# Weight splits a step later on DVE, earlier output half-steps, and hi-first products behind norms, in a fused attention and MoE kernel

## The chip, the cores and the metric

The kernel runs on one core of a Trainium2 chip. The metric is the device time of one execution in microseconds. TensorE (PE) does the matrix products, VectorE (DVE), ScalarE (ACT) and GpSimd (POOL) the rest, and SyncE (SP) issues most of the transfers.

## The reference

All in float32, for 256 tokens of width 1024. It is two blocks in a row.

The first has two layers, each attention and then a gated feed-forward net:

```
layer 0: fox attention, 8 heads (log-sigmoid forget sums added to the scores)
         dsa attention, 8 heads over a latent of 128, top 64 keys picked by an index score
layer 1: moba attention, 16 heads (one block of 256 keys, so plain causal attention here)
each:    x = x + mixed @ w_out;  x = x + (silu(conv3(g)) * u) @ w_down,  g, u = split(rmsnorm(x) @ w_up)
```

The second block is one layer:

```
c_q, c_kv, k_r, x_m, z, i, f = split(rmsnorm(x) @ w_in)
mla attention, 8 heads, from c_q and c_kv
mlstm, 4 heads: xc = silu(conv4(x_m)), q and k from xc, v from x_m, gates i and f
ml = (norm(hm) * g + skip * xc) * silu(z)
x = x + concat(mla, ml) @ w_o
x = x + MoE(rmsnorm(x)), 32 experts, top 2
x = x + (p @ w_ple) * sigmoid(rmsnorm(x) @ w_gate);  return rmsnorm(x)
```

## The kernel before

Five instruction streams are written out by hand, one per engine: `tensor` (PE), `scalar` (ACT), `vector` (DVE), `gpsimd` (POOL) and `sync` (SP). They meet through semaphores only, so the order within each stream is the order of the work. Tokens lie in two tiles of 128 (t = 0, 1); the width of 1024 is eight slices k of 128.

**Products in split precision.** SP brings each weight chunk (up to 1 MB) into a ring of slots. ACT rounds it to `wh` (`split_hi`, line 1249), DVE makes the rest `wl = w - wh` (`split_lo`, line 1757), each into one of three buffers. The other operand is split too: hh and hl of a norm, mh (`mix_hi`, ACT) and ml (`mix_lo`, DVE) of the heads' outputs. PE (line 525) adds three products: high by high, high by low, low by high. A ring slot is free when both splits have read it. `ahead()` is the generator by which ACT and DVE split some chunks ahead of PE.

**A norm.** `add_x` on DVE adds the output projection's banks to x. `norm_T` on PE transposes x (line 529) into four banks of PSUM, two slices k and two tiles t in each, and a bank is announced when it is full. ACT makes hh from it, DVE hl (line 1767). The norms are an0, fn0 (layer 0 and its net), an1, fn1, nm2 (block 2) and np2 (the final gate). `tok_steps` and `gemm_fm` are the products behind a norm; chunk c holds slices k = 2c and 2c+1.

**Head loops.** `for i in range(21)` in layers 0 and 1, `range(15)` in block 2. At step i PE does the scores of head i, a half chunk of the next projection (`next(proj)`), the transposes of head i−2's probabilities (`probs_T`), perhaps another half chunk, and head i−3's value product. `head_at` leaves steps 8 and 9 without a head. DVE does the maxima of step i (lines 1771 and 1762), ACT the exponentials (`probs`, line 1246) and copies of transposed probabilities (`evac_P`). In layers 0 and 1 the first eight heads' outputs are normalised (`finish`), transposed (`mixT`), split, and multiplied by the first half of the output weights in half steps (`out_steps`), while the second eight heads run. Layer 0 also has rotary work on POOL (line 2549) between `even_evac(4)` on ACT and the transposes `dqT` on PE. Block 2's loop mixes mla and mlstm heads; DVE's `ml_1` and `ml_2` are the parts of the latter, and `z_steps` places the half chunks of the z projection. Ahead of it come the products pj and xm, convolution taps on DVE (line 1767, form sA<-sA,cv), copies and Silu.

Banks of PSUM are given out by `claim` and by `take` in a `rotation`; a claim waits until the former content is drained.

## Time and profile before

| what | value |
|---|---|
| median of 3 runs | 1125.15 us (1123.03 to 1128.29) |
| the profiled execution, its time | 1126.01 us |
| its span in the trace | 1124.2 us |
| PE busy | 1056.7 us (94%) |
| DVE busy | 619.9 us (55%) |
| ACT busy | 522.5 us (46%) |
| POOL busy | 89.5 us (8%) |
| mean granted clock of PE | 0.965 |

Times in the trace are microseconds from the start of the span. Stages lie about so: layer 0 to 164, its net to 356, layer 1 to 491, the second net to 683, block 2's attention to 816, router and experts from there to 1090, then the final gate. A span of 40 slices gives PE a busy share of 0.9 or more in most of them; the low ones lie at the start, in the head loops and in block 2.

### The profile page before, as it was taken

To read this page: it belongs to the slowest core of one execution; us is meant where nothing else is said; L and a number is where in the kernel's file an instruction comes from. 1 tells how busy PE (TensorE), PEld (TensorE's weight loads), DVE (VectorE), ACT (ScalarE), POOL (GpSimd) and SP (SyncE) were. 2 spreads that over 40 slices of the span, in tenths; PEclk is the share of its full clock that TensorE was granted. 3 is DMA by queue.
4 is the path that set the end of the run, shared out by engine and by line. 5 is a ranking of instruction groups with operands and counts; after the bars stand their busy time and mean duration, and the time that the engine had idled before them with its cause. 6 is when DMAs were issued, how large, how long until landed. Compare 5 with 4: busy or idle time off the path is not lost.

```text
span 1124.2 us, 15541 instructions
## 1 busy us (share of the span) xinstructions
PE 1056.7 (94%) x6143; PEld 828.0 (74%) x6143; DVE 619.9 (55%) x1167; ACT 522.5 (46%) x901; POOL 89.5 (8%) x104
## 2 busy tenths in 40 slices
PE   6998899999999999999999998888989999999987
PEld 5776679999987877789999887678764544555445
DVE  4667356888845555567888647545672121221146
ACT  5654446555535454455555435655352222222155
POOL 0100000212100311001212101100000000000000
PEclk9998699999999999999999999989889999999989
DMA  8733044465565533246565564105628999999930
GB/s 285 272 113 113 1 142 156 155 200 173 190 199 172 187 118 108 76 133 192 164 192 183 191 186 136 76 13 182 229 107 323 409 409 408 409 409 408 406 129 38
DMA packets 112672, 224.63 MB, mean 200 GB/s; under 512 B 10559, under 2 KB 65234, under 8 KB 112594
## 3 DMA queue, kind: packets, MB, share of 16 engines
q1 hardware_dynamic: 112434, 223.04, 56.3%
q8 instruction: 51, 0.84, 0.3%
q10 hardware_dynamic: 160, 0.53, 0.1%
q14 instruction: 27, 0.22, 0.1%
HBM read 222.50 MB, written 1.05 MB: 199 GB/s over the span
## 4 chain that ended last, share of the span: by engine, by line
PE 81%; DVE 9%; ACT 4%; issue 2%; DMA 2%; SPq 1%; POOL 0%; DVEq 0%; ACTq 0%; POOLq 0%
PE ps L525 76%; PE ps L529 4%; DVE wl L1757 2%; ACT wh L1249 1%; DMA ring<-in_w_uv_dram 1%; DVE smb L1771 1%; DVE x L1757 1%; ACT pb L1246 1%; SPq L2627 1%; DMA ring<-in_w_in_even_dram 1%; DVE sA L1767 1%; DVE xs L1757 0%; DVE hl L1767 0%; SPq L2624 0%; ACT L1246 0%
## 5 line engine op out<-in xcount | busy, mean ns | idle before, releaser
L1757 DVE TENSOR_TENSOR wl<-ring,wh 128x1024 fp32r<-128x1024 f32 (+3 forms) x212 | 278.5, 1323 | 183.2 <-ACT wh L1249 182.5
L1249 ACT ACTIVATE wh<-ring 128x1024 fp32r<-128x1024 f32 (+3 forms) x212 | 222.7, 1053 | 155.5 <-PE ps L525 152.5
L525 PE MATMUL ps<-hh,wh 128*128 128x256 f32 x768 | 220.2, 287 | 3.7 <-DVE big L1762 2.3
L525 PE MATMUL ps<-hh,wl 128*128 128x256 f32 x768 | 217.9, 284 | 0.0
L525 PE MATMUL ps<-hl,wh 128*128 128x256 f32 x768 | 217.9, 284 | 0.0
L525 PEld LDWEIGHTS ps<-hh,wh 128*128 128x128 f32 x768 | 147.9, 193 | 5.0 <-DVE wl L1757 2.6
L525 PEld LDWEIGHTS ps<-hl,wh 128*128 128x128 f32 x768 | 147.9, 193 | 0.3
L525 PEld LDWEIGHTS ps<-hh,wl 128*128 128x128 f32 x768 | 147.9, 193 | 0.0
L525 PE MATMUL ps<-wh,hh 128*128 128x512 f32 (+3 forms) x192 | 81.0, 422 | 6.2 <-DVE wl L1757 4.8
L525 PE MATMUL ps<-ring,xg 128*64 128x512 f32 x320 | 85.5, 595 | 0.0
L2578 POOL TENSOR_TENSOR fs<-fs,rt 128x256 f32<-128x256 f32 x44 | 52.5, 1213 | 331.1 <-ACT fs L1246 331.1
L525 PE MATMUL ps<-wh,hl 128*128 128x512 f32 (+3 forms) x192 | 76.3, 397 | 0.0
L525 PE MATMUL ps<-wl,hh 128*128 128x512 f32 (+3 forms) x192 | 75.9, 395 | 0.0
L1767 DVE SCALAR_TENSOR_TENSOR ysl<-ps,wsl,ysh 128x512 fp32r<-128x512 f32 x32 | 24.0, 750 | 83.0 <-ACT ysh L1246 83.0
L1767 DVE SCALAR_TENSOR_TENSOR fa<-ps,rsl,fs 128x256 f32<-128x256 f32 x16 | 7.7, 484 | 105.7 <-ACT fs L1246 105.7
L525 PEld LDWEIGHTS ps<-ring,xg 128*64 128x64 f32 x320 | 26.4, 137 | 50.4 <-issue 50.2
L1246 ACT ACTIVATE pb<-smb,nbb 128x128 f32<-128x128 f32 x80 | 35.7, 447 | 52.2 <-DVE nbb L1762 52.0
L525 PE MATMUL ps<-ringx,xg 128*64 128x512 f32 x192 | 57.6, 592 | 0.0
L525 PE MATMUL ps<-wh,ffh 128*128 128x512 f32 x176 | 54.9, 389 | 0.0
L525 PE MATMUL ps<-wh,ffl 128*128 128x512 f32 x176 | 54.8, 389 | 0.0
L525 PE MATMUL ps<-wl,ffh 128*128 128x512 f32 x176 | 54.8, 389 | 0.0
L1246 ACT ACTIVATE fs<-ps,rsl 128x256 f32<-128x256 f32 x16 | 7.6, 476 | 101.4 <-PE ps L525 101.4
(273 smaller groups left out, 1731.9 us busy)
## 6 DMA issues: line engine op xcount, KB each, us to landing
ring<-in_w_up_dram SPq DMA_DIRECT2D x88, 512.0 KB, 4.7
ring<-in_w_down_dram SPq DMA_DIRECT2D x22, 1024.0 KB, 4.9
ring<-in_w_gate_e_dram SPq DMA_DIRECT2D x40, 512.0 KB, 7.8
ring<-in_w_up_e_dram SPq DMA_DIRECT2D x40, 512.0 KB, 10.1
ringx<-in_w_down_e_dram SPq DMA_DIRECT2D x16, 1024.0 KB, 9.0
ring<-in_w_down_e_dram SPq DMA_DIRECT2D x16, 1024.0 KB, 10.9
ring<-in_w_in_odd_dram SPq DMA_DIRECT2D x12, 1024.0 KB, 5.0
ringx<-in_w_gate_e_dram SPq DMA_DIRECT2D x24, 512.0 KB, 10.1
```

Source lines behind the costliest of these rows:

```text
L525: return e.matmul(o, l, r, start=start, stop=stop)
L529: return e.transpose(o, i, cst[0:n, C_ID:C_ID + n])
L1246: return e.activation(o, i, f, **kw)
L1249: return e.activation(o, i, ACT.Copy)
L1757: return e.tensor_tensor(o, a, b, op)
L1767: return e.scalar_tensor_tensor(out=o, in0=a, scalar=s, in1=b, op0=o1, op1=o2)
L1771: return e.tensor_tensor_reduce(out=o, in0=a, in1=b, scale=1.0, scalar=init, op0=o1, op1=o2, accum_out=ac)
L2578: e.tensor_tensor(fs[:, f % 2, :], fs[:, f % 2, :], rb, ALU.mult).then_inc(s_silr, 1)
L2627: e.dma_start(dst, src).then_inc(s_c, 16)
```

## The change

It has these parts.

- **Norms.** `norm_T` goes over tile 0 of all four banks first and then tile 1. In the first product behind each norm (`fresh`), chunk 0 does the products with hh for both slices, then those with hl. The norm's banks and those of the products behind it are chosen anew (`norm_banks`, `banks4`).
- **Additions.** DVE's last weight split ahead of `add_x` is moved behind it.
- **Layers 0 and 1.** DVE's `next(proj)` and `next(outp)` come a step later. `even_evac(4)` on ACT moves ahead of `probs(7)`. In layer 0 the value product of head 7 moves to step 9; `finish("fox")`, `mixT`, `mix_hi` and `mix_lo` come at step 10, and the output half-steps at 12 to 16, 18 and 19. In layer 1 they come at step 11 (`mix_lo` at 12) and 13 to 19. `mixed_high` lets the products with mh start when mh is there, and `ready` waits for ml only ahead of the products with ml.
- **Block 2, ahead of the loop.** Splits of chunks 5 and 6 move apart, xm uses other banks, ACT's copies of x move into the splits, `swish` is interleaved with copies, an Exp of one element is done ahead of the aT copies, and the cum2 copy on DVE comes behind two of four groups of taps.
- **Block 2's loop.** `evac_P` comes first in ACT's step, DVE's split comes behind `ml_2` and a step later, the last z half-steps move to 10, 12 and behind the loop, Silu of z behind `mix_hi`, and `gate_rows(3)` is ahead of `mix_lo`.

Cut to its core:

```diff
-z_steps = (0, 2, 4, 6, 8, 9, 10, 11)
+
+out_at = ((12, 13, 14, 15, 16, 18, 19), (13, 14, 15, 16, 17, 18, 19))
+z_steps = (0, 2, 4, 6, 8, 10, 12, 14)
...
     def norm_T(name, ready):
 
-        for i in range(4):
-            for t in range(2):
+
+        for t in range(2):
+            for i in range(4):
                 ready(t, i // 2)
-            b = claim(i, name, i) if name in ("fn0", "fn1") else take(name, i)
-            for j in range(4):
-                k, t = 2 * i + j // 2, j % 2
-                w = tr(b[:, j * P:(j + 1) * P], x[:, t, k * P:(k + 1) * P])
-            w.then_inc(of(full, name, i), 1)
+                if t == 0:
+                    if name in norm_banks:
+                        claim(norm_banks[name][i], name, i)
+                    else:
+                        take(name, i)
+                b = bank[use[name, i][0]]
+                for k in (2 * i, 2 * i + 1):
+                    o = (k % 2) * S + t * P
+                    w = tr(b[:, o:o + P], x[:, t, k * P:(k + 1) * P])
+                if t == 1:
+                    w.then_inc(of(full, name, i), 1)
...
-    def tok_steps(name, norm, c0, width, hh, hl, h2, l2, banks2):
+    def tok_steps(name, norm, c0, width, hh, hl, h2, l2, banks2, fresh=False):
+
 
         for c in range(4):
             wh_, wl_ = weights(c0 + c, h2, l2, 2)
+            if fresh and c == 0:
+                b2 = [claim(banks2[t], name, t) for t in range(2)]
+                for k in range(2):
+                    q.wait_ge(s_hh, hsplit[norm] + k + 1)
+                    for t in range(2):
+                        tk = slice(t * P, (t + 1) * P)
+                        mm(b2[t][:, 0:width], hh[:, k, tk], wh_[:, k, :], k == 0, False)
+                        mm(b2[t][:, 0:width], hh[:, k, tk], wl_[:, k, :], False, False)
+                yield
+                emptied(q, norm, 0)
+                for k in range(2):
+                    for t in range(2):
+                        w = mm(b2[t][:, 0:width], hl[:, k, t * P:(t + 1) * P], wh_[:, k, :], False, False)
+                used.inc(w, c0)
+                chunk_done[c0] = (w_used, used.n)
+                yield
+                continue
             emptied(q, norm, c)
...
                 after()
 
-    def out_steps(name, c0, ks, K, xh_, xl_, ready):
+    norm_banks = {"fn0": (4, 5, 0, 1), "an1": (6, 7, 2, 3), "fn1": (4, 5, 0, 1), "nm2": (6, 7, 2, 3)}
+
+    def out_steps(name, c0, ks, K, xh_, xl_, ready, banks4=(0, 1, 2, 3), high=None):
 
         for k in ks:
             wh_, wl_ = weights(c0 + k, wh, wl)
-            ready(k)
+            (high or ready)(k)
             for t in range(2):
                 tk = slice(t * P, (t + 1) * P)
                 terms = [(a, v, n) for a, v in ((xh_, wh_), (xh_, wl_), (xl_, wh_)) for n in range(2)]
                 if k == K - 1:
                     terms = terms[0::2] + terms[1::2]
                 for a, v, n in terms:
+                    if a is xl_:
+                        ready(k)
                     first = a is xh_ and v is wh_
-                    b = claim(2 * t + n, name, t, n) if k == 0 and first else bank[2 * t + n]
+                    o = banks4[2 * t + n]
...
+    def mixed_high(layer):
+
+        def f(k):
+            if k % 4 < 2:
+                q.wait_ge(s_mhi, 2 * layer + k // 4 + 1)
+            else:
+                emptied(q, (layer, "mixT", k // 4), 1)
+        return f
+
     rotation[:] = [4, 5]
...
+        if i in out_at[0]:
             next(outp)
-        h = head_at.get(i - 3)
+        h = 7 if i == 9 else head_at.get(i - 3) if i != 10 else None
+        if i == 9:
+            emptied(q, "pt", 6)
+            value[0](6)
+            for _ in side:
+                pass
         if h is not None:
             emptied(q, "pt", h)
             if h == 0:
...
         if i < 9:
             next(side, None)
         if i == 9:
-            for _ in side:
-                pass
             q.wait_ge(s_ropep, 3)
             to_T("dqT", [lambda t, g=g: prj[:, t, 1544 + g * P:1544 + (g + 1) * P] for g in range(4)])
-        if i == 12:
+            rotation[:] = [4, 5]
+        if i == 10:
             rotation[:] = [0, 1]
             mixT(0, 0, "fox")
             rotation[:] = [4, 5]
-            outp = out_steps((0, "out"), c_oute, range(4), 8, mh1, ml1, mixed(0))
-    next(outp)
+            outp = out_steps((0, "out"), c_oute, range(4), 8, mh1, ml1, mixed(0), high=mixed_high(0))
     rotation[:] = [4, 5, 6, 7]
     mixT(0, 1, "dsa")
     for _ in outp:
         pass
-    for _ in out_steps((0, "out"), c_oute, range(4, 8), 8, mh1, ml1, mixed(0)):
+    for _ in out_steps((0, "out"), c_oute, range(4, 8), 8, mh1, ml1, mixed(0), high=mixed_high(0)):
         pass
...
-        if i < 10:
+        if i < 12:
             next(proj, None)
-        if 14 <= i < 20:
+        if i in out_at[1]:
             next(outp)
         h = head_at.get(i - 3)
-        if h is not None:
+        if h is not None and h != 7:
...
-        if i == 12:
+        if i == 9:
+            emptied(q, "pt", 16 + 7)
+            value[0](7)
+        if i == 11:
             rotation[:] = [0, 1]
             mixT(1, 0, "moba0")
             rotation[:] = [4, 5]
-            outp = out_steps((1, "out"), c_outo, range(4), 8, mh2, ml2, mixed(1))
-    next(outp)
+            outp = out_steps((1, "out"), c_outo, range(4), 8, mh2, ml2, mixed(1), high=mixed_high(1))
     rotation[:] = [4, 5, 6, 7]
...
             evac_P(h, ptb1)
+        if i == 7:
+            even_evac(4)
         h = head_at.get(i)
         if h is not None:
             probs(h, h, 0.125, smb1, pb1)
         next(proj, None)
-        if i in (2, 7):
-            even_evac(3 if i == 2 else 4)
+        if i == 2:
+            even_evac(3)
         if i < 5:
             next(proj, None)
-        if 14 <= i < 20:
+        if i in out_at[0]:
...
         act(xcT[:, 2 * m:2 * m + 2, :], xcT[:, 2 * m:2 * m + 2, :], ACT.Silu).then_inc(s_xc, 1)
+
     q.wait_ge(s_xn, 2)
     for t in range(2):
         evac(mix[:, t, 512:1024], "mv", t)
+    swish(0)
     for i in (1, 3):
         evac(flat(qT3[0:96, 2 * i:2 * i + 2, :]), "q2T", i, rows=96)
-    filled(q, "q2T", 3)
+    swish(1)
+    act(st[:, 60:61], cst[:, C_ONE:C_ONE + 1], ACT.Exp)
     for g in range(2):
         evac(aT(0, g), "abT", 0, g, rows=2)
     for h in range(4):
...
         act(mk[:, h, :], b[:, S:2 * S], ACT.Copy, scale=float(128.0 ** -0.5)).then_inc(of(drained, "mqk", h), 1)
     proj = ahead(c_in2[2], 4)
     for i in range(15):
+        if 2 <= i < 14:
+            evac_P(32 + i - 2, ptb3)
         if i < 12:
...
             for h in range(4):
                 act(xcT[:, h, :], xcT[:, h, :], ACT.Copy, scale=gain("sk2", h))
-        if i == 13:
-            for m in range(4):
-                emptied(q, "z", m)
-            act(szT[:, :, :], szT[:, :, :], ACT.Silu).then_inc(s_sz, 1)
     mix_hi(2, 0, mh3)
+    for m in range(4):
+        emptied(q, "z", m)
+    act(szT[:, :, :], szT[:, :, :], ACT.Silu).then_inc(s_sz, 1)
     q.wait_ge(s_var, RV["mln"])
...
+            finish("fox", 8, lambda t: mix[:, t, 0:512])
         h = head_at.get(i)
         if h is not None:
             maxima(h, h, MA if h < 8 else dsam, 0.125, smb1)
-        if 3 <= i < 10:
+        if i < 10:
             next(side, None)
-        if i == 11:
-            finish("fox", 8, lambda t: mix[:, t, 0:512])
-        next(proj, None)
-        if i < 5:
+        if i >= 1:
             next(proj, None)
-        if 14 <= i < 20:
+        if 1 <= i < 6:
+            next(proj, None)
+        if i - 1 in out_at[0]:
             next(outp)
         if i < 3:
             next(side, None)
-            next(side, None)
-        if i == 12:
+        if i == 10:
             filled(q, ("even", 4), 1)
             mix_lo(0, 0, mh1, ml1, 1)
             outp = ahead(c_oute, 4)
...
     mix_lo(0, 1, mh1, ml1, 2)
     for _ in outp:
         pass
-    for k in range(4, 8):
+    for k in range(4, 7):
         split_lo(c_oute + k + 3, wh, wl)
     add_x((0, "out"))
+    split_lo(c_ffn[0] + 2, wh, wl)
 
     def ffn(l):
         c0 = c_ffn[l]
...
                 split_lo(c0 + 4 * s + c + 3, wh, wl)
                 if s and c != 1:
                     (conv, None, gate, split)[c](s - 1)
-        for j in range(18):
+        for j in range(17):
             split_lo(c0 + 4 * 12 + j + 3, wh, wl)
         add_x(("ffo", l))
+        split_lo(c0 + 4 * 12 + 20, wh, wl)
 
...
+        h = head_at.get(i - 2)
+        if h is not None and h % 2 == 0:
+            evac_P(16 + h, ptb2)
+        if i >= 1:
+            next(proj, None)
+            next(proj, None)
+        if i in (3, 7, 11):
+            n = (i + 9) // 4
+            tok_evac(("odd", n), big2[:, 0, ODD[n]:ODD[n] + 512], "an1")
+        if i - 1 in out_at[1]:
...
     for i in (0, 2):
         evac(kT3[0:64, 2 * i:2 * i + 2, :].rearrange("p h s -> p (h s)"), "kT2", i, rows=64)
-    for m in range(4):
+    def taps(m):
         q.wait_ge(s_cv2, m + 1)
         for k in range(3):
             w = stt(xcT[:, m, :], xmT[:, m, k:k + S], gain("cw2", 4 * k + m), xcT[:, m, :], ALU.mult, ALU.add)
...
                 own.inc(w)
         if m % 2:
             w.then_inc(s_xcp, 1)
+
+    taps(0)
+    taps(1)
     b = filled(q, "cum2")
     f4 = b[:, 0:8].rearrange("p (t h d) -> p t h d", t=2, d=1)
     own.inc(cp(ab[:, :, :, 0:1], f4))
...
     tt(ab[:, :, :, 3:4], ig.unsqueeze(3), ab[:, :, :, 0:1], ALU.subtract).then_inc(s_ab, 1)
...
+    def gate_rows(m):
+        b = filled(q, "z", m)
+        tt(szT[:, m, :], b[:, 0:S], rb, ALU.mult).then_inc(of(drained, "z", m), 1)
+
...
-        if i in z_steps:
-            next(proj)
         if 1 <= i <= 12 and order2[i - 1][0] == "ml":
             ml_2(order2[i - 1][1], 32 + i - 1)
-        if i in z_steps[1::2]:
-            m = z_steps.index(i) // 2
-            b = filled(q, "z", m)
-            tt(szT[:, m, :], b[:, 0:S], rb, ALU.mult).then_inc(of(drained, "z", m), 1)
+        if i - 1 in z_steps:
+            next(proj)
+        if i in z_steps[1:7:2]:
+            gate_rows(z_steps.index(i) // 2)
         if 10 <= i < 13:
             next(hms)
     q.wait_ge(s_xn, 2)
     finish("mla", 8, lambda t: mix[:, t, 0:512])
-    filled(q, "z", 3)
+    gate_rows(3)
     mix_lo(2, 0, mh3, ml3, 5)
     for _ in hms:
         pass
```

## Rows read from the trace of the kernel before

**Rows 1.** Windows: length, busy (count) of PE, PEld, DVE, ACT, POOL, PEclk, DMA, GB/s.
```profile
62.00:170.00 108.00, 95.23 (x471) 75.01 (x470) 60.61 (x175) 51.61 (x121) 3.08 (x6) 0.87 0.28 88
353.00:496.00 143.00, 135.07 (x690) 108.40 (x689) 81.03 (x166) 71.32 (x142) 17.75 (x24) 0.99 0.40 132
683.00:741.00 58.00, 50.70 (x298) 42.78 (x298) 36.37 (x84) 38.01 (x65) 8.76 (x13) 0.94 0.22 78
741.00:788.00 47.00, 39.26 (x260) 35.26 (x259) 25.23 (x95) 23.46 (x64) 0.97 (x1) 0.90 0.40 122
...
842.00:1090.00 248.00, 241.70 (x1240) 115.70 (x1240) 55.27 (x93) 57.97 (x127) 0.00 (x0) 1.00 0.95 375
89.00:96.00 7.00, 6.59 (x17) 4.69 (x18) 6.10 (x21) 2.56 (x7) 0.00 (x0) 0.51 0.25 65
108.00:117.00 9.00, 3.91 (x22) 3.03 (x21) 2.86 (x9) 4.08 (x10) 3.08 (x6) 0.77 0.37 117
113.40:133.30 19.90, 16.57 (x61) 12.37 (x62) 7.74 (x31) 7.61 (x25) 0.56 (x2) 0.50 0.00 1
758.00:761.40 3.40, 3.40 (x15) 3.10 (x16) 1.01 (x6) 1.29 (x3) 0.00 (x0) 0.50 0.97 389
785.30:794.90 9.60, 7.72 (x23) 6.00 (x23) 7.34 (x11) 4.68 (x6) 2.35 (x1) 0.50 0.85 303
```

**Rows 2.** Timeline around fn0: start, length, instruction, idle before and its releaser.
```profile
166.58 1.94 PE L529 MATMUL ps<-cst,x 128*128 128x128 f32 x16 [1.57 <-DVE x L1757]
169.29 0.35 PE L525 MATMUL ps<-hh,wh 128*128 128x256 f32 x1 [0.77 <-DVE hl L1767]
...
164.55 2.47 DVE L1757 TENSOR_TENSOR x<-x,ps 128x512 f32<-128x512 f32 x4
...
167.32 3.03 ACT L1246 ACTIVATE hh<-ps,cv 128x256 fp32r<-128x256 f32 x8 [2.43 <-PE ps L529]
```

**Rows 3.** Timeline at the final gate's norm, PE and ACT.
```profile
1089.93 3.65 PE L529 MATMUL ps<-cst,x 128*128 128x128 f32 x16 [2.40 <-issue]
...
1091.06 3.40 ACT L1246 ACTIVATE hh<-ps,cv 128x256 fp32r<-128x256 f32 x8 [2.82 <-PE ps L529]
```

**Rows 4.** Timeline of PE in layer 0's loop.
```profile
89.41 2.07 PE L525 MATMUL ps<-ring,sA 128*128 128x512 f32 x2 [2.63 <-DVE mxb L1771]
...
114.10 1.97 PE L529 MATMUL ps<-cst,big 128*128 128x128 f32 x8 [2.38 <-POOL big L2549]
...
124.21 1.94 PE L529 MATMUL ps<-cst,xs 128*128 128x128 f32 x8 [1.86 <-DVE xs L1757]
```

**Rows 5.** Timeline of DVE in layer 0's loop.
```profile
83.67 1.21 DVE L1757 TENSOR_TENSOR wl<-ring,wh 128x1008 fp32r<-128x1008 f32 x1 [3.13 <-ACT wh L1249]
...
126.57 0.69 DVE L1757 TENSOR_TENSOR ml<-ps,mh 128x512 fp32r<-128x512 f32 x1 [1.63 <-ACT mh L1249]
```

**Rows 6.** Timeline of ACT and POOL ahead of dqT.
```profile
109.18 1.23 ACT L1246 ACTIVATE big<-ps,rin 128x504 f32<-128x504 f32 x2
...
110.57 2.41 POOL L2549 TENSOR_TENSOR sA<-big,trig 128x128 f32<-128x128 f32 x4 [69.63 <-ACT big L1246]
```

**Rows 7.** Timeline of PE in layer 1's loop.
```profile
456.45 0.92 PE L525 MATMUL ps<-kT,qT 64*128 64x128 f32 x4 [2.41 <-DVE mxb L1771]
```

**Rows 8.** Timeline of PE, DVE and ACT in block 2.
```profile
698.60 0.36 PE L525 MATMUL ps<-hh,wh 128*128 128x256 f32 x1 [2.27 <-DVE big L1762]
...
730.17 0.65 PE L529 MATMUL ps<-cst,big 128*96 128x128 f32 x4 [2.89 <-DVE st L1775]
...
757.02 0.89 PE L525 MATMUL ps<-fs,big 2*128 2x128 f32 x4 [2.63 <-DVE rs L1771]
...
722.39 7.44 DVE L1767 SCALAR_TENSOR_TENSOR sA<-sA,cv 128x256 f32<-128x256 f32 x12
...
739.50 1.28 ACT L1246 ACT_TABLE_LOAD   x1
740.79 0.40 ACT L1246 ACTIVATE pb<-smb,nbb 128x128 f32<-128x128 f32 x1
```

More of the change, by code:

```diff
@@ L941, in tensor @@
                 pass
-            for _ in out_steps((1, "out"), c_outo, range(4, 8), 8, mh2, ml2, mixed(1)):
+            for _ in out_steps((1, "out"), c_outo, range(4, 8), 8, mh2, ml2, mixed(1), high=mixed_high(1)):
                 pass
@@ L979, in tensor @@
             side = side2()
-            gemm_fm("xm", "nm2", c_in2[1], hh3, hl3, wh, wl, (0, 1, 2, 3), lambda: next(side, None))
+            gemm_fm("xm", "nm2", c_in2[1], hh3, hl3, wh, wl, (2, 3, 0, 1), lambda: next(side, None))
             for _ in side:
@@ L1075, in tensor @@
                     value[n](h)
+            next(zp)
             rotation[:] = [4, 5, 6, 7]
             mixT(2, 0, "mla")
-            for _ in out_steps((2, "out"), c_outm, range(0, 3), 8, mh3, ml3, mixed(2)):
+            for _ in out_steps((2, "out"), c_outm, range(0, 3), 8, mh3, ml3, mixed(2), high=mixed_high(2)):
                 pass
@@ L1547, in scalar @@
             q.wait_ge(s_rstd, RV["nm2"])
[L1548 to L1549 removed]
+            split_hi(c_in2[0] + 6, wh)
             tok_evac("pj", pj[:, 1, :], "nm2", 424)
@@ L1584, in scalar, with swish @@
             for t in range(2):
-                act(x[:, t, :], xs[:, t, :], ACT.Copy, scale=rinv_of("mid", t)).then_inc(s_xn, 1)
-            for t in range(2):
                 evac(v2[:, t, :, :].rearrange("p h d -> p (h d)"), "v2", t)
-            for m in range(2):
+            def swish(m):
                 q.wait_ge(s_xcp, m + 1)
@@ L2191, in vector @@
                 pass
-            for k in range(4, 8):
+            for k in range(4, 7):
                 split_lo(c_outo + k + 3, wh, wl)
             add_x((1, "out"))
+            split_lo(c_ffn[1] + 2, wh, wl)
             ffn(1)
```

77 lines of the change are left out of this document (42 added, 35 removed).

## The prediction

> **What bounds the kernel now.** I read the page's shares first, then windows stage by stage, then the timelines of PE, DVE and ACT around every idle gap of PE. TensorE is busy in nearly all of the span, so a change can pay in two places only: where PE stands still, and where it works at half clock. The windows [rows 1] give both for the stages that the diff touches. Idle is length minus busy: 12.8 us in 62 to 170, 7.9 in 353 to 496, 7.3 in 683 to 741, 7.7 in 741 to 788. Where the granted clock is 0.50 (1.2 of 2.4 GHz) a busy microsecond gives half: 16.57 busy in 113.4 to 133.3 lose 8.3, 6.59 at 0.51 in 89 to 96 lose 3.2, 7.72 in 785.3 to 794.9 lose 3.9, and each stretch such as 758 to 761.4 loses 1.7. Nearly all the low stretches begin after PE waited over 2 us. The MoE stage, 842 to 1090, is the rest that counts: PE busy 241.7 of 248 at full clock and DMA 0.95. The diff leaves it alone, PE reaches it with the weight ring full, and so it should move earlier as a block. About 60 us in all, idle and clock together, are within reach.
>
> **Boundaries.** At fn0 PE waits 1.57 for x, does 16 transposes in 1.94, and waits 0.77 for hl [rows 2]. The four additions (2.47, so 0.62 each) stand behind a weight split on DVE (1.21 for such a one, [rows 5]); putting it behind `add_x` lets them start about 1.3 sooner; the split is needed only by a later chunk, where by my count its margin shrinks from 2 us to 0.6. The transposes then begin about 1.6 sooner. The first chunk's new order needs only hh (3.03 for 8, 0.38 each), no longer hl, which DVE makes from hh; that is most of the 0.77. Together about 2.4, at fn0, an1 and fn1, whose rows have the same form with waits within 0.1: **+7.1** after 0.1 for the later split. Bounds: 5 (only the split moved) and 7.8. The same `norm_T`, now tile by tile, has a price at the end of the kernel. There 16 transposes at half clock take 3.65, and ACT's first hh came 1.13 behind their start, when four were done, because a bank was then full [rows 3]. Now a bank is full after ten, and ACT's chain, then PE, starts some 0.9 to 1.3 later: **−0.9**. At the start of the kernel PE waits for weights by DMA anyway: 0.
>
> **Layer 0's loop, up to the ninth score.** PE waits 2.63 at 89.41 for a maximum [rows 4]. That maximum is behind a split on DVE that itself had waited 3.13 for ACT's wh [rows 5]: the lag of a step puts the split behind the maxima and takes that wait off. The next, 108 to 117, is 5.1 us idle [rows 1]: rope on POOL waited for `even_evac(4)` on ACT, and PE for rope [rows 6, 4]. `even_evac(4)` moves ahead of probs(7). With 0.8 of small waits (12.8 less 2.63, 5.09, 2.34 and 1.86, of rows 1, 4 and 2), 3.2 of low clock at 89 and 0.9 at 108 to 117 (3.91 busy at 0.77), 12.6 us go. New or left: probs_T(7) waits about 1.1, since two evacuations (1.23) are now ahead of probs(7); rope about 0.9; the dqT evacuation 0.75; value(7), which moves ahead of the score, 0.6. That is 3.3: **+9.3**. Bounds: 5 if only the wait at 89.41 and its clock go, 12.6.
>
> **Layer 0's loop, behind it.** Before: a wait of 1.86 for mixed output at 124.21 and about 7.3 of clock behind 117 (8.3 less its share before), 9.2 in all. Now `finish("fox")`, mixT and both mix parts come at step 10 and outputs from 12. probs_T(8) has to wait for a chain: two DVE maxima ops (1.4 at 0.69), two of probs (1.2), mix_hi 0.6, three ops of mix_lo at 0.69 [rows 5] (2.1), and 0.7 for maxima(9) queued behind them, 6.0, against 2.8 of PE work (mixT 0.97, half of its 1.94 at half clock, a score 0.92 and as much again). 3.2 stay idle. `finish("dsa")` at the end has no half step of the output over it any more: 1.2. The clock I take as recovered in the main, with 2.8 left, because this stretch still consists of short pieces between waits: 9.2 − 7.2 = **+2.0**. Bounds: −0.6 (all of the clock loss of 5.4 stays) and +4.8. The Trainium skill bears on this bound (TensorE: Matmul & The Clock Gate, Part 4, "PE-mode transpose"): transposes don't count as busy for the clock the way matmuls do, and by that the low clock would last over mixT and dqT, and the term would be near its lower end. The trace agrees so far that the clock was 0.50 from the transposes at 114.1 on, but matmuls in that stretch had it too.
>
> **Cost of the lag.** Each split lands a step later. DVE is busy 60.6 of 108 us in the first window and 81 of 143 in the second, a split takes 1.2, and chunks are split ahead, so I cost it 0. The ring's slot is released as much later; DMA is at 0.28 to 0.40 there, which hides SP's refill. Without that cover each late split costs PE what it is late, and the low clock after it.
>
> **Layer 1's loop.** Idle without the boundaries is 7.9 − 4.5 = 3.4; the largest, 2.41, is a score behind maxima(11) that stood behind mix_lo [rows 7]. The new order trades it for a wait of probs_T(9) on `evac_P(8)` behind mix_lo (1.8), an unprotected `finish` (0.75), and 0.9 of old small ones: equal. Of the low clock behind the old wait (1.7, as in block 2) I take half: **+0.8** (0 to 2.5).
>
> **Into block 2.** nm2 is a fourth boundary without new arithmetic ahead of it: +2.0. The xm product waits 2.27 at 698.60 for DVE's pj evacuation behind two splits [rows 8]; one of them now follows, and other banks come first, 1.5 left; with 0.5 of clock: **+3.3** (2.8 to 4.5).
>
> **Before its loop.** PE waits 2.89 at 730.17 for the cum2 copy, which is behind 12 convolution taps of 7.44 in all [rows 8]; now behind six. But the product mqk has to wait for aT's evacuation, now behind swish(1) and the Exp warm-up, a table load of 1.28 [rows 8]. By my count that evacuation lands where it did, near 735.2. So the idle time moves and no more, and a wait of over 3 us ahead of a dense stretch brings a low stretch: **−1.7** (−1.8 to 0). On this the Trainium skill (ScalarE: Activation LUTs, "What ACT_TABLE_LOAD costs") says about 1.28 us for a load and some 1.38 of drain. The rows show the 1.28, and ACT's next instruction begins 0.01 us behind its end. By the page the term would be −3.1.
>
> **Block 2's loop.** Seven waits make 7.7 us: 2.63 at 757.02 [rows 8], where ml_2 stood behind a split of the pattern of rows 5, another of the same kind, and five of 0.4 to 1.0. With the split behind ml_2 and evac_P first on ACT I leave 1.6; 6.1 go, and of two low stretches of 1.7 nearly all, 3.0: **+9.1** (6 to 9.5). The Silu on sz moves behind mix_hi and costs nothing there.
>
> **Tail.** In 785.3 to 794.9 PE is idle 1.9 and loses 3.9. The outputs' high products no longer wait for mix_lo, but the fourth gate row (0.4) is now ahead of it, and soon after PE waits for DVE's and ACT's chain hm, mlo, mh, ml whatever it did before: **+1.3** (0.5 to 2).
>
> **Sum.** 7.1 − 0.9 + 9.3 + 2.0 + 0.8 + 3.3 − 1.7 + 9.1 + 1.3 = 30.3 us. The profiled execution took 1126.0 (its span 1124.2 and 1.8 around it), the median of the runs is 1125.15, 0.9 lower. 1126.0 − 30.3 = 1095.7; as a median **1094.8 us**, 2.7% faster. A difference below about 0.5% (5.6 us) could not be told from none.
>
> **Rivals.**
> *Only the fixed waits go.* The loops re-form: each removed wait comes back one operation later, because the chain score, maxima, probs, transposes is as long as before. Then boundaries 7.1, xm 3.3, 2.63 at 89.41 with its clock, less 2.6 of losses, and a third of block 2's loop, give 16.6: 1108.5. For it speaks that layer 1's idle by my own count is unchanged.
> *The clock comes back as well.* All upper bounds: boundaries 7.8, layer 0 12.6 + 4.8, layer 1 2.5, 4.5, 0, 9.5, 2, less 0.9 are 42.8: 1082. Against it: 2 to 3 us waits remain in all three loops.
> *Slower: the lagged split starves PE.* Some 26 chunks pass through the three loops. If the split of each lands behind the moment when PE wants its wl product, PE stands still at that place, and DVE's backlog never shrinks. To lose the 30.3 and 5.6 more it takes 1.4 us per chunk (36/26). For it: a split does wait up to 3.1 us now, and steps without a projection half leave less cover. Against: DVE is idle over 40% of those windows. At that point: 1131.
> *Nothing comes out.* MoE could be set by DMA (0.95) and start when data does, not when PE does. But PE is 97% busy in it, the ring is full before it, and DMA stands at 0.28 to 0.40 ahead. With the end's −0.9 it would give about 1126.
>
> **Chances.** The forecast's case 0.62, only the fixed waits 0.22, the clock as well 0.09, nothing 0.03, slower 0.04. The likeliest case by its own bounds is 1086 to 1104. To leave out no more than 2 in 10, the range reaches to most of the rivals at either side: 1081 to 1113. Faster by over 0.5% 0.93, within it 0.03, slower 0.04.
>
> **What would show it.** Right: at fn0, an1 and fn1 from the last output matmul to the first product 2.4 less, hh·wh first; no wait by a maximum behind a wl near 89 us; in the window of the ninth score under 3 us idle; clock near 1.0 from there to the end of the loop; block 2's loop idle under 2 us; the tail's 16 transposes followed by hh about a microsecond later. Wrong: PE waits with wl as releaser in the loops (the lag), a low clock over layer 0's second half (then about 1098 to 1100), mqk earlier than 735.2 less the shift (then 2 better), or a MoE stage that has become longer.

## The result, and the profile after

The changed kernel takes 1097.3 us (median of 4, 1093.0 to 1098.86) against 1124.7 before: ratio 0.9746, interval 0.9708 to 0.9785. Run once more unedited (e5_again below) it took 1098.5, ratio 0.9766 (0.9736 to 0.9796). The forecast was 1094.8, with 1081 to 1113. So 27.4 us were measured where 30.3 were forecast.

The profiled execution took 1093.0, span 1090.9; that is 33.0 less than the profiled one before, more than the medians give. PE's clock goes some way to explain it: its mean granted clock was 0.983 in this execution and 0.975, 0.978 and 0.981 in the three timed ones. What follows is therefore read stage by stage, and stages whose length hangs on the clock are named.

Windows of the changed kernel, columns as in [rows 1]. The stages are those of before, moved to where they now lie; 104 to 118 is the stretch around the ninth score, 711 to 716 the product mqk.

```profile
60.00:156.00 96.00, 89.50 (x478) 71.97 (x477) 60.08 (x173) 50.12 (x118) 3.80 (x6) 0.93 0.28 91
341.00:479.00 138.00, 134.48 (x695) 108.55 (x694) 81.33 (x165) 70.38 (x142) 15.87 (x24) 0.99 0.38 124
663.00:719.00 56.00, 50.86 (x306) 42.55 (x305) 37.60 (x86) 39.73 (x70) 9.96 (x13) 0.97 0.24 80
719.00:757.00 38.00, 35.28 (x253) 32.51 (x253) 24.98 (x94) 20.47 (x59) 0.00 (x0) 0.94 0.47 138
811.00:1057.00 246.00, 240.30 (x1232) 114.90 (x1228) 55.05 (x92) 57.08 (x124) 0.00 (x0) 1.00 0.96 378
104.00:118.00 14.00, 10.11 (x37) 7.37 (x37) 5.02 (x19) 5.59 (x17) 0.92 (x3) 0.51 0.19 63
711.00:716.00 5.00, 4.79 (x15) 3.96 (x16) 0.00 (x0) 2.10 (x7) 0.00 (x0) 0.66 0.00 0
```

Idle time (length less busy) is now 6.5 us in layer 0's window instead of 12.8, 3.5 instead of 7.9 in layer 1's, 5.1 instead of 7.3 and 2.7 instead of 7.7 in block 2's two. The clock went from 0.87 to 0.93 in the first window and from 0.90 to 0.94 in block 2's loop. MoE is as busy as before (240.3 of 246 us, 241.7 of 248 before) and simply starts 30 us sooner.

Timeline of PE, DVE and ACT around fn0 in the changed kernel (answers to [rows 2]).

```profile
153.40 1.91 PE L531 MATMUL ps<-cst,x 128*128 128x128 f32 x16
155.39 0.35 PE L527 MATMUL ps<-hh,wh 128*128 128x256 f32 x1
155.58 0.28 PE L527 MATMUL ps<-hh,wl 128*128 128x256 f32 x1
...
151.56 2.73 DVE L1825 TENSOR_TENSOR x<-x,ps 128x512 f32<-128x512 f32 x4 [1.02 <-PE ps L527]
...
154.20 1.22 DVE L1825 TENSOR_TENSOR wl<-ring,wh 128x1024 fp32r<-128x1024 f32 x1
...
155.71 3.23 DVE L1835 SCALAR_TENSOR_TENSOR hl<-ps,cv,hh 128x256 fp32r<-128x256 f32 x8 [0.29 <-ACT hh L1310]
```

No idle time stands in brackets at PE any more: the transposes follow the last output product (153.17) at once, and the first products use hh alone while DVE is still making hl (from 155.71 on). From the last output product to the first product it was 4.68 us and is 2.22.

Timeline of PE in the loops, every wait over 0.3 us from 60 us to 785 us (to [rows 4, 7, 8]).

```profile
101.64 0.55 PE L531 MATMUL ps<-cst,pb 128*128 128x128 f32 x3 [1.03 <-ACT pb L1310]
105.14 1.97 PE L531 MATMUL ps<-cst,big 128*128 128x128 f32 x8 [1.49 <-POOL big L2625]
107.88 1.62 PE L527 MATMUL ps<-sA 64*128 64x128 f32 x4 [0.78 <-ACT sA L1313]
114.97 0.88 PE L531 MATMUL ps<-cst,pb 128*128 128x128 f32 x3 [1.98 <-DVE mxb L1839]
140.01 1.25 PE L531 MATMUL ps<-cst,xs 128*128 128x128 f32 x8 [1.14 <-DVE xs L1825]
...
435.37 0.92 PE L527 MATMUL ps<-kT,qT 64*128 64x128 f32 x4 [0.38 <-DVE mxb L1839]
438.08 0.52 PE L531 MATMUL ps<-cst,pb 128*128 128x128 f32 x3 [1.80 <-DVE ptb L1843]
461.87 1.25 PE L531 MATMUL ps<-cst,xs 128*128 128x128 f32 x8 [1.07 <-DVE xs L1825]
...
677.59 0.39 PE L527 MATMUL ps<-hh,wh 128*128 128x256 f32 x1 [1.25 <-DVE big L1830]
706.70 1.47 PE L531 MATMUL ps<-cst,sA 128*2 128x128 f32 x12 [0.86 <-ACT big L1313]
711.21 5.38 PE L527 MATMUL ps<-sA,ring 128*128 128x256 f32 x16 [3.03 <-ACT big L1313]
723.60 0.89 PE L527 MATMUL ps<-big 2*128 2x128 f32 x4 [0.79 <-DVE rs L1839]
752.76 1.54 PE L527 MATMUL ps<-big,ptb 128*128 128x64 f32 x6 [1.92 <-ACT ptb L1313]
758.98 0.97 PE L527 MATMUL ps<-wh,mh 128*128 128x512 f32 x2 [0.31 <-issue]
767.33 0.72 PE L527 MATMUL ps<-wh,mh 128*128 128x512 f32 x2 [2.38 <-DVE wl L1825]
774.34 0.70 PE L527 MATMUL ps<-wh,mh 128*128 128x512 f32 x2 [0.33 <-DVE ml L1825]
```

Most new waits are those that the forecast had named: the three ahead of the ninth score (1.03, 1.49 and 0.78), 1.98 for its chain, 1.14 and 1.07 for an uncovered `finish`, 1.80 in layer 1, 3.03 at mqk. The waits of 1.92 at 752.76 and 2.38 at 767.33 had not been seen coming.

Stage by stage, each the difference of the start times of the same two instructions in both profiled executions (the last stage ends with the end of PE's last product):

| stage | before | after | gain | forecast |
|---|---|---|---|---|
| start, to the weights at 47 us | 46.85 | 47.76 | −0.9 | 0 |
| to the ninth score | 69.99 | 60.12 | 9.9 | 9.3 |
| to the last output product of layer 0 | 47.77 | 45.29 | 2.5 | 2.0 |
| boundaries fn0, an1, fn1 | 13.83 | 6.50 | 7.3 | 7.1 |
| layer 1, between its boundaries | 130.51 | 130.62 | −0.1 | 0.8 |
| nm2, pj and xm, to the product at 722.37 before | 39.72 | 35.15 | 4.6 | 3.3 |
| from there to the first score of block 2 | 16.25 | 17.27 | −1.0 | −1.7 |
| block 2's loop | 47.77 | 40.35 | 7.4 | 9.1 |
| its outputs | 29.08 | 28.34 | 0.7 | 1.3 |
| router and MoE | 271.68 | 269.70 | 2.0 | 0 |
| final gate, to PE's last product | 29.40 | 28.42 | 1.0 | −0.9 |

Part of the gain up to the ninth score lies ahead of the loop. Eight products of one form mark the place in every profile; these are the kernel before, the changed one, and two experiments below, e7_lag_alone and e8_mask_first:

```profile
68.00 2.47 PE L525 MATMUL ps<-sA 128*128 128x256 f32 x8
67.39 2.47 PE L527 MATMUL ps<-sA 128*128 128x256 f32 x8
71.07 2.47 PE L525 MATMUL ps<-sA 128*128 128x256 f32 x8
65.95 2.47 PE L525 MATMUL ps<-sA 128*128 128x256 f32 x8
```

From the weights at 47 us to here it took 21.2 before and 19.6 after, because PE was at half clock for 3.4 us behind its wait of 2.16 at the weights before and not at all behind 1.27 after. Only the rest of the way, 48.84 before and 40.49 after, is the loop's: 8.4 of the 9.9.

### The profile page after: what moved, and what is told of

Its sections match the earlier page's. It is cut to its first block, busy times and chain, and to the rows that moved or that the text cites. A ratio compares the mean times of both kernels' runs of the same rounds, so it can differ in the third digit from the quotient of the medians.

```text
span 1090.9 us, 15541 instructions
## 1 busy us (share of the span) xinstructions
PE 1040.6 (95%) x6143; PEld 816.4 (75%) x6143; DVE 621.6 (57%) x1167; ACT 521.4 (48%) x902; POOL 90.2 (8%) x104
## 4 chain that ended last, share of the span: by engine, by line
PE 89%; DVE 6%; ACT 2%; DMA 1%; issue 1%; POOL 0%; SPq 0%; DVEq 0%; POOLq 0%; ACTq 0%
PE ps L527 84%; PE ps L531 5%; DVE wl L1825 1%; DMA ring<-in_w_uv_dram 1%; ACT hh L1310 1%; DMA cst<-in_const_dram 0%; DVE hl L1835 0%; DVE ml L1825 0%; ACT wh L1313 0%; DVE xs L1825 0%; DVE smb L1839 0%; POOL sA L2625 0%; DVE sA L1835 0%; ACT L1310 0%; ACT sA L1310 0%
## 5 line engine op out<-in xcount | busy, mean ns | idle before, releaser
L527 PE MATMUL ps<-hl,wh 128*128 128x256 f32 x768 | 215.5, 284 | 0.0
L527 PE MATMUL ps<-wh,hl 128*128 128x512 f32 (+3 forms) x192 | 73.6, 391 | 0.0
L1839 DVE CUSTOM_DVE_ANT_0 smb<-ps,cst 128x128 f32<-128x128 f32 x72 | 25.7, 357 | 44.3 <-PE ps L527 42.7
```

Of the source, the lines that this page charges most:

```text
L527: return e.matmul(o, l, r, start=start, stop=stop)
L1839: return e.tensor_tensor_reduce(out=o, in0=a, in1=b, scale=1.0, scalar=init, op0=o1, op1=o2, accum_out=ac)
```

## Experiments

In each run the kernel before ran beside it on the same chip. The two nets between the boundaries took 186.85 us each, within 0.02, in every profile, before, after and in all experiments, so what differs lies in the other stages.

**e1_no_lag.** The changed kernel, DVE's splits back at their old steps.

```diff
-                if i >= 1:
-                    next(proj, None)
-                if 1 <= i < 6:
-                    next(proj, None)
-                if i - 1 in out_at[0]:
+                next(proj, None)
+                if i < 5:
+                    next(proj, None)
+                if i in out_at[0]:
...
+                if i in z_steps:
+                    next(proj)
                 if 1 <= i <= 12 and order2[i - 1][0] == "ml":
                     ml_2(order2[i - 1][1], 32 + i - 1)
-                if i - 1 in z_steps:
-                    next(proj)
```

> The changed kernel with DVE's weight splits back at their old steps in the three head loops (the rest of the change stays). My theory, by the waits of the kernel before: the wait of 2.6 us for a maximum near 89 us and the low clock behind it (3.2) come back, and in block 2's loop the waits of 1.6 and 2.6 with 3.4 of low clock, so about 12 us more than the changed kernel, near 1109. Rival (the waits go with the other moves, the lag is a detail): under 3 us more, 1097 to 1100.

1109.8 us (1107.5 to 1118.9), ratio 0.9882 (0.9815 to 0.9949). By the medians the size is as my theory had it (12.5 more than the changed kernel), the place is not. The stretch to the ninth score took 59.7, no longer than with the lag; layer 1 took 130.7, the same. It came back in block 2's loop, which took 55.9 instead of 40.4, and 8 more than before the change. (The profiled execution was 18.9 above the changed kernel's; besides the loop's 15.5 it lost some 4 in outputs, MoE and gate, where nothing was edited.) PE and DVE in that loop, then PE near 85 us:

```profile
736.40 0.89 PE L527 MATMUL ps<-fs,big 2*128 2x128 f32 x4 [3.75 <-DVE rs L1839]
754.87 0.80 PE L531 MATMUL ps<-cst,pb 128*128 128x128 f32 x3 [3.00 <-DVE rs L1839]
...
734.35 1.23 DVE L1825 TENSOR_TENSOR wl<-ring,wh 128x1024 fp32r<-128x1024 f32 x1 [3.94 <-ACT wh L1313]
...
85.21 1.12 PE L527 MATMUL ps<-ring,sA 128*128 128x512 f32 x2 [0.94 <-DVE mxb L1839]
```

The split waits 3.94 us for ACT's wh, and ml_2 stands behind it. Near 85 us only 0.9 of the old 2.6 is there, so something else in the change had taken that wait off.

**e2_late_out.** The changed kernel, outputs of layers 0 and 1 at their old steps, lag kept.

```diff
-        out_at = ((12, 13, 14, 15, 16, 18, 19), (13, 14, 15, 16, 17, 18, 19))
+        out_at = ((14, 15, 16, 17, 18, 19, 20), (14, 15, 16, 17, 18, 19, 20))
...
-                if i == 10:
+                if i == 12:
                     rotation[:] = [0, 1]
                     mixT(0, 0, "fox")
```

> The changed kernel with finish, mixed transposes, their splits and the output half-steps of layers 0 and 1 back at their old steps (11, 12, 14 to 20), the lag kept. My theory: the term behind the ninth score was 2.0 and that of layer 1 0.8, so 2 to 3 us more, the difference lying between 108 and 153 us. Rival (the earlier outputs are what ended the low clock of the second half): 7 to 9 us more, with a clock of 0.5 over some 20 us. Second rival (they only trade waits): no difference.

1098.9 us (1095.3 to 1101.6), ratio 0.9779 (0.9734 to 0.9824); by the time alone no different from the changed kernel. In the profile layer 0 behind the ninth score took 48.0 instead of 45.3, and layer 1 133.6 instead of 130.6. Layer 1's part shows mostly in two waits, 1.28 and 3.48 where the changed kernel has 0.38 and 1.80:

```profile
437.68 0.92 PE L527 MATMUL ps<-kT,qT 64*128 64x128 f32 x4 [1.28 <-DVE mxb L1839]
442.09 0.88 PE L531 MATMUL ps<-cst,pb 128*128 128x128 f32 x3 [3.48 <-DVE ptb L1843]
```

In layer 1 the earlier outputs are worth 3.0 against the lagged order and nothing against the old one. In layer 0 the 2.7 is clock and not waiting: PE stood still no longer than in the changed kernel, but the clock was near 0.50 until some 17 us behind the ninth score, against 10. That length also moves where nothing in the stretch was edited. Kernels with the changed kernel's code there took 44.0 (e3_old_norms) and 47.0 (e4_two_norms), the old code took 47.8 (before) and 50.8 (e10_evac_first), and e11_best and e12_best2, alike there, took 50.1 and 45.9. So the 2.7 is near the forecast's 2.0, but it is no larger than what the clock does by itself, and is not shown to come from the outputs.

**e3_old_norms.** The changed kernel with the transposes bank by bank in all norms, `fresh` off, and each last split ahead of `add_x`.

```diff
-                for t in range(2):
-                    for i in range(4):
...
+                order = [(t, i) for t in range(2) for i in range(4)]
+                if name in ('an0', 'an1', 'fn0', 'fn1', 'nf2', 'nm2', 'np2'):
+                    order = [(t, i) for i in range(4) for t in range(2)]
...
-                    if fresh and c == 0:
+                    if False:
...
-            for k in range(4, 7):
+            for k in range(4, 8):
                 split_lo(c_oute + k + 3, wh, wl)
             add_x((0, "out"))
-            split_lo(c_ffn[0] + 2, wh, wl)
```

> The changed kernel with the old order in all norms: bank by bank, the first chunk as the others, and the last split ahead of the additions (banks as in the changed kernel). My theory: 2.4 at each of fn0, an1 and fn1 and 2.1 at nm2 come back (9.3), the start gains 0.9 and the final gate 0.9, so about 7.5 more, near 1105. Rival (what the norms give is taken back behind them by splits that arrive later): 3 us or less.

1101.5 us (1099.7 to 1102.9), ratio 0.9789 (0.9745 to 0.9833), 4 more than the changed kernel. In the profile the three boundaries took 13.0 (4.4, 4.3, 4.3) instead of 6.5, so 2.2 each, and nm2 4.0 instead of 2.1. But the stretch from pj to the product that ends the row of the table was 1.4 shorter, without the wait of 1.25 at xm. At nm2 the new order gives 1.9 and takes back 1.4, because pj's evacuation on DVE comes later. These stages add up to 7.0, the medians to 4; why the medians show less is open, since the clock moved other stages of this profile both ways.

**e4_two_norms.** The same order of the transposes for an0 and np2 alone.

```diff
+                order = [(t, i) for t in range(2) for i in range(4)]
+                if name in ('an0', 'np2'):
+                    order = [(t, i) for i in range(4) for t in range(2)]
```

> The changed kernel with the old bank-by-bank order in two norms only, the first (an0) and that of the final gate (np2). My theory after the result: the tile-by-tile order costs 0.9 at each, so the first product behind the load of weights at 47.8 us comes 0.9 sooner and ACT's first hh comes 0.6 to 1.2 us sooner behind the last transposes: 1.8 less, near 1095.5. Rival, as forecast (the start waits for a transfer anyway): nothing at the start, 0.9 at the end.

1096.8 us (1096.4 to 1097.8), ratio 0.9754 (0.9711 to 0.9798), by the time alone no different from the changed kernel. At the gate, transposes to first product took 2.66 instead of 3.31: the forecast's 0.9 is 0.65 at full clock. At the start nothing came sooner; the weights were ready at 48.4 instead of 47.8, and PE, waiting 3.7 for them, lost 2.3 more to a low clock behind the wait (62.4 to the ninth score instead of 60.1).

**e5_again.** No edit.

> The changed kernel once more, unedited, as the base for the other kernels of this set. By my reading of the profiles the stages between the loops repeat to 0.1 us; the time at which the weights at 47 us are ready and the length of layer 0's second half vary by 1 to 3 us with the clock. Expected 1096 to 1098; in its profile the wait at 47 us is again under 1.5 us and the clock behind it full.

1098.5 us (1092.8 to 1106.0), ratio 0.9766 (0.9736 to 0.9796). Every stage of its profile is within 0.05 us of the first profile of the changed kernel, up to the router. Again the profiled execution was the fastest one of its kernel, 5.7 us below the median (4.3 the first time).

**e6_all.** The changed kernel with four moves more.

```diff
+                if name in ('np2',):
+                    order = [(t, i) for i in range(4) for t in range(2)]
...
+            for g in range(2):
+                evac(aT(0, g), "abT", 0, g, rows=2)
             swish(1)
             act(st[:, 60:61], cst[:, C_ONE:C_ONE + 1], ACT.Exp)
-            for g in range(2):
-                evac(aT(0, g), "abT", 0, g, rows=2)
...
-                if i == 12:
-                    q.wait_ge(s_xc, 2)
-                    for h in range(4):
-                        act(xcT[:, h, :], xcT[:, h, :], ACT.Copy, scale=gain("sk2", h))
+            q.wait_ge(s_xc, 2)
+            for h in range(4):
+                act(xcT[:, h, :], xcT[:, h, :], ACT.Copy, scale=gain("sk2", h))
             mix_hi(2, 0, mh3)
...
+            split_lo(c_outm + 3, wh, wl)
             for _ in hms:
                 pass
```

> The changed kernel with four moves more: the bank-by-bank order back at the final gate's norm alone; ACT's copies of aT ahead of the second swish; ACT's four scaled copies of block 2 moved behind the loop; one split of the output weights on ACT and DVE ahead of the wait for the head norm. My theory: 0.65 at the gate, up to 3.0 at mqk and 1.8 of low clock behind it, 1.5 of the wait of 1.9 near 753, 2.4 at 767, with 1 to 2 of clock: 8 less than the changed kernel. Rival (each wait is followed by another one on DVE's chain): 3 less or none; then the waits turn up again at the third mqk product and at the first ml product behind the hm transposes.

1091.5 us (1088.3 to 1094.2), ratio 0.968 (0.9654 to 0.9706), 7.0 below e5_again of the same set. Block 2 in its profile:

```profile
710.82 3.72 PE L527 MATMUL ps<-sA,ring 128*128 128x256 f32 x16 [0.95 <-ACT sA L1312]
749.15 0.88 PE L527 MATMUL ps<-big,ptb 128*128 128x64 f32 x6 [0.34 <-ACT ptb L1315]
759.48 0.73 PE L527 MATMUL ps<-wh,mh 128*128 128x512 f32 x2 [0.18 <-DVE wl L1826]
763.81 1.09 PE L531 MATMUL ps<-cst,xs 128*128 128x128 f32 x8 [1.32 <-DVE xs L1826]
770.41 1.19 PE L527 MATMUL ps<-wh,mh 128*128 128x512 f32 x2 [2.43 <-DVE ml L1826]
```

The early copies of aT took the wait at mqk from 3.03 to 0.95, and the product ran in 3.72 instead of 5.38, at full clock: 3.7 in all. The scaled copies behind the loop took 1.92 to 0.34, and the loop was 2.9 shorter. The tail split is the rival's case: 2.38 for wl became 0.18, and 1.32 and 2.43 appeared behind it, because hm's chain on DVE now stood behind that split. The outputs took 30.8 instead of 28.3.

**e7_lag_alone.** The kernel before with the lag and nothing else (the same lines as in e1_no_lag, the other way, in all three loops).

> The kernel before with the lag of DVE's splits in the three loops and nothing else. My theory: the maxima at 89 us is no longer behind a split that waits (2.6 and 3.2 of clock), block 2's loop loses its waits of 1.6 and 2.6 with 3.4 of low clock, so 12 less than before, near 1112. Rival (the lag pays only in company: it took the mask work ahead of the splits in layer 0, evac_P first in block 2): 4 less or nothing.

1105.4 us (1103.3 to 1112.5), ratio 0.9802 (0.9772 to 0.9832). The lag alone is worth 20 of the 27 us by medians. Its profiled execution was its slowest, 13.6 less than the profiled one before; it had PE wait 3.8 us at the weights near 48 us, with half clock behind it, and a low clock in layer 1 (2.2 us more there). In it the ninth score was 7.6 nearer, and 8.9 nearer (40.0 instead of 48.8) when counted from the products at 71.07, without the low clock at the weights. Block 2's loop took 39.1 instead of 47.8, at a clock of 1.00:

```profile
741.00:775.00 34.00, 30.68 (x236) 28.36 (x235) 22.68 (x89) 20.78 (x56) 0.33 (x1) 1.00 0.53 165
```

**e8_mask_first.** The kernel before with one DVE step of the mask ahead of the splits, no lag.

```diff
-                if 3 <= i < 10:
+                if i < 10:
                     next(side, None)
...
                 if i < 3:
                     next(side, None)
-                    next(side, None)
```

> The kernel before with one DVE step moved and no lag: in layer 0's first three steps one of the two steps of the top-64 mask stands ahead of the splits instead of behind them. Theory from the run without the lag, where the wait near 89 us had shrunk from 2.6 to 0.9 with a full clock: the mask work fills the time in which the split waits for ACT, so the wait shrinks to 0.9 and the low clock of 89 to 96 us is gone, 5 less, near 1120. Rival (the lag did it): the wait stays at 2.6 and the time at 1124 to 1125.

1121.8 us (1114.3 to 1126.4), ratio 0.9964 (0.9944 to 0.9984). PE and DVE near 84 us:

```profile
84.42 1.12 PE L525 MATMUL ps<-ring,sA 128*128 128x512 f32 x2 [0.94 <-DVE mxb L1771]
...
80.38 1.21 DVE L1757 TENSOR_TENSOR wl<-ring,wh 128x1008 fp32r<-128x1008 f32 x1 [2.65 <-ACT wh L1249]
```

The split still waits, but mask work that used to stand between it and the maxima is done already, and the wait of PE is 0.94. To the ninth score it took 62.5, 7.5 less than before, but 1.5 of that is the clock at the weights, which stayed full behind a wait of 1.96. From the products at 65.95 it took 42.9, so the edit gave 6.0 where the lag alone gave 8.9. Either edit takes most of that wait off, and both together (the changed kernel, 8.4, with one value product more ahead of the score) give it once. The profiled execution was also the fastest of its kernel, 7.4 below the median; by medians the edit is worth 4.

**e9_an0_alone.** The kernel before with the tile-by-tile order in an0 only (the loop of the changed `norm_T`, for that name).

> The kernel before with the tile-by-tile order in the first norm (an0) alone. My theory from the runs so far: the products ahead of 47 us come about 1.8 us later while the weights at 47 us land when they did, so PE waits 1.3 there instead of 2.2 to 3.8, the low clock of 48 to 52 us is gone and the stretch from 47 us to the ninth score shrinks from 70.0 to 67.7: 2.3 less. Rival (forecast): nothing; second rival: the wait stays and PE is 0.9 later.

1124.8 us, ratio 0.9992 (0.9979 to 1.0005). My theory fell: PE waited 3.06 at 48.48 and the low clock came as before. In all the profiles of this study the weights at that place were ready between 46.3 and 48.7 us, in no relation to the norm's order. DVE stood there for the transfer of w_uv (5.4 to 7.0 us in the profiles before, after and of this run), so the start is set by the transfer, and the 0.9 lost there in the profiled execution is scatter. The order does shorten PE's wait, since the first product of the kernel comes 1.0 to 1.7 us later with it (13.9 to 14.2 against 12.5 to 12.8): a low clock followed in two of eight profiles with the new order and in five of six with the old. Whether that difference is more than chance is not shown; this run's time gives it no worth.

**e10_evac_first.** The kernel before with ACT's evac_P first in each step of block 2's loop.

```diff
             for i in range(15):
+                if 2 <= i < 14:
+                    evac_P(32 + i - 2, ptb3)
                 if i < 12:
...
-                if 2 <= i < 14:
-                    evac_P(32 + i - 2, ptb3)
```

> The kernel before with ACT's evac_P first in each step of block 2's loop and nothing else. My theory from the run without the lag, whose loop took 55.9 us against 47.8 before: evac_P first makes ACT wait for PE's transposes ahead of the exponentials and wh, the DVE splits wait with it, and the loop grows to about 56: 8 us more, near 1133. Rival, as forecast (evac_P first shortens the waits): the loop shrinks by 1 to 2.

1130.7 us (1128.1 to 1132.9), ratio 1.0043 (1.0028 to 1.0057): slower by 5.6. The loop took 54.3 instead of 47.8, at a clock of 0.82. Window, then PE, DVE and ACT:

```profile
741.00:793.00 52.00, 42.27 (x253) 37.93 (x253) 24.88 (x95) 23.10 (x63) 0.00 (x0) 0.82 0.34 105
...
759.73 0.89 PE L525 MATMUL ps<-fs,big 2*128 2x128 f32 x4 [3.75 <-DVE rs L1771]
...
757.68 1.22 DVE L1757 TENSOR_TENSOR wl<-ring,wh 128x1024 fp32r<-128x1024 f32 x1 [3.79 <-ACT wh L1249]
...
755.35 0.49 ACT L1249 ACTIVATE ptb<-ps 128x384 f32<-128x384 f32 x1 [3.81 <-PE ps L529]
```

Read from below: ACT waits 3.81 for PE's transposes at evac_P, only then makes wh, the split waits 3.79 for it, ml_2 stands behind the split, and PE waits 3.75 for ml_2's result.

**e11_best.** The changed kernel with e6_all's moves without the tail split, mix_lo a step later in layer 0, evac_P ahead of mix_lo in layer 1, and pj without `fresh`.

```diff
-                if i == 10:
+                if i == 11:
                     filled(q, ("even", 4), 1)
                     mix_lo(0, 0, mh1, ml1, 1)
...
-            gemm_tok("pj", "nm2", c_in2[0], 424, hh3, hl3, wh, wl, (0, 1), True)
+            gemm_tok("pj", "nm2", c_in2[0], 424, hh3, hl3, wh, wl, (0, 1))
```

> The changed kernel with six edits: the bank-by-bank order at the final gate, ACT's aT copies ahead of the second swish, ACT's scaled copies behind block 2's loop (as in the run before, without its tail split), mix_lo behind the maxima of step 11 in layer 0, evac_P ahead of mix_lo in layer 1, and the first product of block 2 without hi-first. Theory: 1.5 to 2.0 at the ninth head's transposes and 1.8 at layer 1's, 1.3 at xm less 0.7 at nm2, 2.4 at the tail against the run before: 1085 to 1088. Rival (the head chain moves the waits one step on): same as the run before, 1091.

1091.2 us (1090.4 to 1092.9), ratio 0.9698 (0.968 to 0.9715), no better than e6_all: the rival. In layer 0 the wait of 1.98 became 0.94 and then 0.47 for ml, in layer 1 1.80 became 1.29 for ml. nm2 took 3.5 instead of 2.1 and xm did not wait: even. The tail's outputs took 27.9.

**e12_best2.** The same with evac_P at its old place in block 2.

> The same, and ACT's evac_P at its old place in block 2's steps. Theory: the loop took 40.35 with evac_P first and 39.1 with the lag alone, so another 1.2 less in the loop. Rival: the place no longer matters once the copies are behind the loop, no difference.

1089.9 us (1087.6 to 1092.9), ratio 0.9697 (0.9677 to 0.9716). The loop took 37.9 against 37.4, so nothing was to be had there. Of the versions tried these three are the fastest, 1090 to 1091.5, and I can't tell them apart; all lie below the changed kernel, by 5 to 9 us (ratios of 0.968 to 0.970 against 0.975 and 0.977).

## Why the prediction was right, and where it was not

**Where the time is lost and what bounds it.** Right: nothing was gained in the nets, and idle and clock account for the rest. MoE moved as a block; its 2.0 and the gate's 1.0 in the profiled execution are clock. The stage of router and MoE, edited nowhere, took 269.7 in five of the profiles and 270.9 to 272.3 in the other nine.

**Boundaries.** Right, 7.3 for 7.1, confirmed stage by stage from the other side by e3 (6.5), though its medians differ by 4 only. The part at nm2 was counted at 2.0 and is 0.5 net, since it brings back a wait at xm.

**Gate.** The step is right and its size is 0.65 instead of 0.9 (e4); in the profiled execution full clock hid it: the transposes took 1.97 and the first product still began 3.31 behind their start, as it had at half clock before.

**Layer 0 up to the ninth score.** The size came out (9.9 for 9.3) partly by luck: 1.5 of it is the clock behind the weights at 47 us, which the forecast had put at nothing, and the loop gave 8.4. The waits left ahead of the score are 3.3 where 2.75 was forecast (rope's is 1.49 and not 0.9). The reason was incomplete. I put the removed 2.63 and its low clock down to the lag. The lag alone does that (8.9, e7), but so, for the most part, does the mask step moved ahead of the splits (6.0, e8), which I had not costed; without the lag the changed kernel loses nothing there (e1).

**Behind it.** 2.0 forecast, 2.5 in the profile, 2.7 by e2; but the same code gave 44.0 to 47.0 in this stretch, a gain of 0.8 to 3.8 on the kernel before, so that the size came out so near is not to the forecast's credit. The chain that I added up to a stall of 3.2 stalled PE for 1.98, at half clock, where PE's own work covers more. On the Trainium skill's sentence (TensorE: Matmul & The Clock Gate, Part 4, "PE-mode transpose"): in the window of 104 to 118 the clock was 0.51 from dqT on, but it was back by 118, over ordinary matmuls and single transposes, and 16 transposes at each boundary ran in 1.91 without a drop behind them. No lasting loss of the kind that I had bounded at 5.4 appeared in this kernel. It did in e11_best, where the clock stayed at 0.50 until 20 us behind the score and the stretch took 50.1; what decides between the two is open.

**Cost of the lag.** Costed at nothing, right: PE waits for wl nowhere in the three loops. Its worth was misplaced. By e7 it is the greater part of the change.

**Layer 1.** Right that waits are traded; the half of a low clock was not gained.

**Into block 2.** 4.6 for 3.3: the low clock behind xm (0.50 from 701 to 703 before) went fully. **Before its loop.** Right to the place: the wait at mqk is 3.03, and the product behind it lost 1.76 to the clock (5.38 against 3.62); −1.0 for −1.7, since mqk still came 0.7 sooner. The load of the table took 1.28 at 709.09 and ACT's next instruction began at 710.38. The further 1.38 which the Trainium skill gives (ScalarE: Activation LUTs, "What ACT_TABLE_LOAD costs") does not show, as before, and the row decides.

**Block 2's loop.** The step that failed in its reasoning: I counted evac_P first among the gains. By itself it costs 6.5 (e10), and only the lag makes it harmless: with the copies moved as well the loop took 37.4 with it and 37.9 without (e11, e12). The lag alone gave 8.7. That 7.4 came of 9.1 lies mostly in the wait of 1.92 behind the four scaled copies, which were worth 2.9 when moved (e6).

**Tail.** 0.7 for 1.3, by the wait of 2.38 for wl, which I had not seen.

**Signs.** Of the signs of being right, three came only in part: 3.3 us stayed idle ahead of the ninth score instead of under 3, the clock was low until 118 and only then near 1.0, and block 2's loop stood idle 2.7 us instead of under 2.

What stays open: the medians fell by 27.4 and the profiled executions by 33.0, 5.6 more. The stretches whose clock alone changed hold about 4.5 (MoE 2.0, gate 1.0, and 1.5 behind the weights at 47 us). That the timed executions lack just these is argued from their lower mean clock and not shown, since only one execution per kernel has a trace.

## What to carry to other kernels

When an engine prepares operands for another in a loop, ask what waits behind a preparation that itself waits: a split that came a step too early held up the maxima behind it, and moving it one step later in all three loops, at no cost to its consumer, was worth 20 us. Two edits can each remove the same wait, so credit needs each tried alone, and compared over a stretch that begins behind any other change of the clock. And an order that is harmless with slack on the next engine (evac_P first) can cost more than it ever gave when that slack is missing.

## What the runs showed of the hardware that was not expected

A wait of PE of 1.7 to 3.8 us at the weights near 47 us was followed by 3 to 7 us at half clock in seven of the profiles, one of 1.96 was not, and none of 1.3 or less was. From the weights to the eight products of 2.47 it took 19.6 us where the clock stayed full and 21.2 to 22.5 where it did not. So such a wait cost 1.5 to 2.8 us again in clock. The clock also moves a stage that nobody edited: the second half of layer 0 by 3 to 4 us, router and MoE by up to 2.6. And the profiled execution of a kernel can lie 4 to 7 us below its median (the changed kernel twice, with stage lengths that repeat to 0.05 us up to the router, and e8_mask_first) or 7 above it (e7_lag_alone). So a wait is best read in the profile, a small gain only where the clock of the stage is alike on both sides, and the sum in the timed runs.
